# Cross attention's scores as three products of high and low parts instead of one f32 product

## The reference

```python
kv = (mem @ mem_w_kv).astype(jnp.float32)
mem_k = kv[..., :D_MODEL].reshape(B, MEM_LEN, XATTN_HEADS, XATTN_HD)   # 4 heads of 256
mem_v = kv[..., D_MODEL:].reshape(B, MEM_LEN, XATTN_HEADS, XATTN_HD)

def memory_cross_attn(x, mem_k, mem_v, wq, wo):
    q = (x @ wq).reshape(B, S, XATTN_HEADS, XATTN_HD).astype(jnp.float32)
    s = jnp.einsum('bshd,bmhd->bhsm', q, mem_k) * (XATTN_HD ** -0.5)
    p = jax.nn.softmax(s, axis=-1)
    o = jnp.einsum('bhsm,bmhd->bshd', p, mem_v).reshape(B, S, D_MODEL)
    return o @ wo
```

## Time and profile before

| | us |
|---|---|
| median of 3 runs | 960.01 |
| lowest, highest | 959.79, 960.27 |
| run that was profiled | 960.27 |
| its span, from the first to the last instruction | 958.4 |
| TensorE busy | 945.1 (99%) |
| VectorE busy | 685.7 (72%) |
| ScalarE busy | 517.9 (54%) |
| GpSimd busy | 54.5 (6%) |

### The profile page before, as it was taken

The page is one execution under the profiler, slowest core; times in us unless marked ns, Lnnn a source line. Parts: engine busy times, 40 slices in busy tenths (PEclk is TensorE's granted clock), DMA queues, the critical chain, the costliest instruction groups (busy, mean ns, idle before and its releaser), DMA issues.

```text
span 958.4 us, 12980 instructions
## 1 busy us (share of the span) xinstructions
PE 945.1 (99%) x5064; PEld 811.6 (85%) x5064; DVE 685.7 (72%) x933; ACT 517.9 (54%) x732; POOL 54.5 (6%) x96
## 2 busy tenths in 40 slices
PE   9999999999999999999999999998999999999997
PEld 8889888888888888888788888887988888888885
DVE  6966578658888775975788777668677886556555
ACT  6756563526655555264275555547466575444543
POOL 0000121001000002100100000002100000000000
PEclk9999999999999999999999999999999999999998
DMA  9975275527989885183299798763631565655521
GB/s 330 330 252 176 88 273 203 206 88 258 336 273 300 288 289 206 50 312 127 88 317 332 272 305 290 245 224 131 229 130 47 176 223 195 216 179 186 176 78 45
DMA packets 109516, 203.00 MB, mean 212 GB/s; under 512 B 4188, under 2 KB 75120, under 8 KB 106128
## 3 DMA queue, kind: packets, MB, share of 16 engines
q1 hardware_dynamic: 105856, 189.15, 58.2%
q0 software_dynamic: 3168, 12.24, 3.6%
q10 hardware_dynamic: 432, 0.79, 0.2%
HBM read 201.09 MB, written 1.06 MB: 211 GB/s over the span
## 4 chain that ended last, share of the span: by engine, by line
PE 90%; DVE 6%; ACT 2%; issue 1%; DMA 1%; POOL 0%; SPq 0%; POOLq 0%; DVEq 0%; ACTq 0%
PE WB L362 20%; PE YB L387 11%; PE YB L380 10%; PE YB L395 10%; PE WB L365 10%; PE YB L441 4%; PE WB L380 2%; PE WB L344 2%; PE WB L387 2%; PE WB L395 2%; PE WB L351 2%; PE WB L347 2%; PE WB L696 1%; PE WB L715 1%; PE WB L479 1%
## 5 line engine op out<-in xcount | busy, mean ns | idle before, releaser
L1713 DVE TENSOR_TENSOR wl<-raw,wh 128x2048 fp32r<-128x2048 f32 (+1 forms) x146 | 334.3, 2296 | 117.6 <-ACT wh L1103 115.2
L1103 ACT CAST wh<-raw 128x2048 fp32r<-128x2048 f32 (+1 forms) x150 | 285.3, 1905 | 33.7 <-PE YB L395 8.9
L362 PE MATMUL WB<-XS,wh 128*128 128x512 f32 x832 | 208.1, 392 | 0.0
L362 PEld LDWEIGHTS WB<-XS,wh 128*128 128x128 f32 x832 | 152.2, 188 | 29.1
L365 PEld LDWEIGHTS WB<-XS,wl 128*128 128x128 f32 x832 | 113.5, 190 | 8.2
L365 PE MATMUL WB<-XS,wl 128*128 128x256 f32 x832 | 116.0, 282 | 0.0
L380 PE MATMUL YB<-wh,FHT 128*128 128x512 f32 x352 | 109.0, 391 | 0.0
L387 PE MATMUL YB<-wl,FHT 128*128 128x512 f32 x352 | 108.6, 390 | 0.0
L395 PE MATMUL YB<-wh,FLT 128*128 128x512 f32 x352 | 108.5, 389 | 0.0
L1279 ACT COPY U<-WB 128x256 f32<-128x256 f32 x102 | 33.1, 376 | 132.8 <-PE WB L365 132.8
L387 PEld LDWEIGHTS YB<-wl,FHT 128*128 128x128 f32 x352 | 66.1, 188 | 14.1
(11 more groups left out here) (339 smaller groups left out, 1205.8 us busy)
## 6 DMA issues: line engine op xcount, KB each, us to landing
raw<-in_mlp_w SPq DMA_DIRECT2D x64, 1024.0 KB, 5.2
raw<-in_w_ada_t SPq DMA_DIRECT2D x24, 1024.0 KB, 4.9
raw<-in_mlstm_w_in SPq DMA_DIRECT2D x11, 1024.0 KB, 9.0
raw<-in_w_ffn_down SPq DMA_DIRECT2D x11, 1024.0 KB, 5.0
raw<-in_w_ffn_gate SPq DMA_DIRECT2D x10, 1024.0 KB, 5.4
raw<-in_w_ffn_up SPq DMA_DIRECT2D x10, 1024.0 KB, 5.6
raw<-in_mem_w_kv SPq DMA_DIRECT2D x8, 1024.0 KB, 5.2
raw<-in_xattn_wq SPq DMA_DIRECT2D x8, 1024.0 KB, 7.1
```

What stands on the lines that cost most here:

```text
L362: e.matmul(W[:, :], H[:, at(k)], XS[:, k, :], start=k == 0, stop=False)
L1103: f = e.copy(w[:, 0:a * b], raw[:, 0:a * b])
L1713: f = e.tensor_tensor(L[:, 0:a * b], raw[:, 0:a * b], H[:, 0:a * b].bitcast(F32), ALU.subtract)
```

## The change

Scores are computed from high and low parts: high query by high key, high query by low key, low query by high key, all in fp32r and added up in one PSUM bank. For that

- the keys are kept as `KH` and `KL_` in the place of `KV` (a new name `KHL` of type fp32r for the same memory). ScalarE's copy of the keys becomes a cast into `KH`; VectorE computes `KL_` by a new subtraction from the bank (`key_low`, line 1881 of the new file), and it is this that gives the bank back. `VM` moves to columns 2048 to 4095 of `AR`, two bias buffers to columns 4096 to 6143;
- ScalarE's copy of the queries of heads 0 and 1 becomes a cast into `FH`; those of heads 2 and 3 get a new cast behind the join (`high`, line 1312). VectorE gets a new subtraction for each head (`query_low`, line 2055);
- on ScalarE the copy of the turned head 1 stands ahead of the exponentials of head 2; on VectorE the conversion of the third `wo` chunk (`q(3)`) stands behind the scores of head 3.

```diff
-        KT = KV[:, 0:2048].rearrange("p (k c) -> p k c", k=8)
-        VM = KV[:, 2048:4096].rearrange("p (t c) -> p t c", t=2)
+        KH, KL_ = (KHL[:, 2048 * n:2048 * n + 2048].rearrange("p (k c) -> p k c", k=8) for n in range(2))
+        VM = AR[:, 2048:4096].rearrange("p (t c) -> p t c", t=2)
...
@@ TensorE
                 def scores(h):
                     W = bank(("xs", i, h))
-                    e.wait_ge(*act_mlstm["mv", 1, 1])
-                    e.wait_ge(*(act_xa if h < 2 else dve_xa)["q", i, h])
-                    Q = halves(QT[h])
+                    e.wait_ge(*dve_mlstm["mk", 3])
+                    e.wait_ge(*act_xa["qh", i, h])
+                    H, L = halves(FH[h % 2]), halves(FL[h % 2])
                     for t in range(2):
+                        o, tk = W[:, 256 * t:256 * t + 256], slice(128 * t, 128 * t + 128)
                         for f in range(2):
-                            p = e.matmul(W[:, 256 * t:256 * t + 256], Q[:, f, 128 * t:128 * t + 128],
-                                         KT[:, 2 * h + f, :], start=f == 0, stop=f == 1)
+                            e.matmul(o, H[:, f, tk], KH[:, 2 * h + f, :], start=f == 0, stop=False)
+                        for f in range(2):
+                            e.matmul(o, H[:, f, tk], KL_[:, 2 * h + f, :], start=False, stop=False)
+                        e.wait_ge(*dve_xa["ql", i, h])
+                        for f in range(2):
+                            p = e.matmul(o, L[:, f, tk], KH[:, 2 * h + f, :], start=False, stop=f == 1)
                     p.then_inc(pe_xa.add(("s", i, h)))
...
@@ ScalarE
-                e.copy(KT[:, 2 * j:2 * j + 2, :], halves(W[:, :])).then_inc(act_mlstm.add(("mk", j)))
-                freed["mk", j] = act_mlstm["mk", j]
+                e.copy(KH[:, 2 * j:2 * j + 2, :], halves(W[:, :])).then_inc(act_mlstm.add(("mk", j)))
...
-                        e.copy(QT[h], W[:, :]).then_inc(act_xa.add(("q", i, h)))
+                        e.copy(FH[h], W[:, :]).then_inc(act_xa.add(("qh", i, h)))
...
+                def high(h):
+                    e.wait_ge(*dve_xa["q", i, h])
+                    e.wait_ge(*pe_xa["s", i, h - 2])
+                    e.copy(FH[h % 2], QT[h]).then_inc(act_xa.add(("qh", i, h)))
...
                 hi_to(M["wq", i, 3] + 3)
+                high(2)
                 scores(0)
                 q(3)
                 turned(0)
                 scores(1)
+                high(3)
+                turned(1)
                 scores(2)
                 values(0)
-                turned(1)
                 scores(3)
...
@@ VectorE
+            def key_low(j):
+                W = bank_of.get(("mk", j), WB[0])
+                e.wait_ge(*act_mlstm["mk", j])
+                e.tensor_tensor(KL_[:, 2 * j:2 * j + 2, :], halves(W[:, :]),
+                                KH[:, 2 * j:2 * j + 2, :].bitcast(F32), ALU.subtract
+                                ).then_inc(dve_mlstm.add(("mk", j)))
+                freed["mk", j] = dve_mlstm["mk", j]
...
             lo_to(M["mk", 1] + 3)
+            key_low(0)
             head_c(0)
+            key_low(1)
             lo_to(M["mk", 2] + 3)
-            head_a(2)
+            decays(2)
+            key_low(2)
+            weighted(2)
             head_c(1)
             lo_to(M["mk", 3] + 3)
             head_a(3)
             head_c(2)
             lo_to(M["mv", 0, 1] + 3)
+            key_low(3)
             head_c(3)
...
+                def query_low(h):
+                    e.wait_ge(*act_xa["qh", i, h])
+                    e.tensor_tensor(FL[h % 2], QT[h] if h > 1 else YB[2 + h][:, :], FH[h % 2].bitcast(F32),
+                                    ALU.subtract).then_inc(dve_xa.add(("ql", i, h)))
+
-                for h in range(3):
-                    q(h)
+                q(0)
+                query_low(0)
+                q(1)
+                query_low(1)
+                q(2)
                 query(2)
                 scores(0)
-                q(3)
+                query_low(2)
                 query(3)
                 scores(1)
+                query_low(3)
                 scores(2)
                 values(0)
                 scores(3)
+                q(3)
                 values(1)
```

More of the change, by code:

```diff
@@ L182, in build_program @@
         XH, XL = XS[:, :, 0:256], XS[:, :, 256:512]
+        with nc.sbuf_tensor("KHL", [128, 4096], F32R) as KHL:
+            pass
         KV = sb("KV", [128, 4096])
@@ L188, in build_program @@
         FL = [FLT[:, 512 * i:512 * i + 512] for i in range(2)]
-        BV = [sb(f"bv{i}", [128, 1024]) for i in range(2)] + [AR[:, 1024:2048], AR[:, 2048:3072]]
+        BV = [sb(f"bv{i}", [128, 1024]) for i in range(2)] + [AR[:, 4096:5120], AR[:, 5120:6144]]
         IDN = sb("IDN", [128, 128])
@@ L232, in build_program @@
         CT = [S[:, 2 * n:2 * n + 2, :].rearrange("p k c -> p (k c)") for n in range(2)]
-        KT = KV[:, 0:2048].rearrange("p (k c) -> p k c", k=8)
-        VM = KV[:, 2048:4096].rearrange("p (t c) -> p t c", t=2)
+        KH, KL_ = (KHL[:, 2048 * n:2048 * n + 2048].rearrange("p (k c) -> p k c", k=8) for n in range(2))
+        VM = AR[:, 2048:4096].rearrange("p (t c) -> p t c", t=2)
         TMP = AR[:, 6144:8800]
-        QT = [TMP[:, 512 * n:512 * n + 512] for n in range(2)] + [U[:, 0, 512 * n:512 * n + 512] for n in range(2)]
+        QT = [None, None] + [U[:, 0, 512 * n:512 * n + 512] for n in range(2)]
         PART = [U[:, 1, 512 * n:512 * n + 512] for n in range(2)] * 2
@@ L711, in values @@
                     W = bank(("xv", i, h))
+                    e.wait_ge(*act_mlstm["mv", 1, 1])
                     e.wait_ge(*act_xa["pt", i, h])
@@ L724, in free @@
                 def free(t, nb):
-                    return act_xa["q" if t else "ct", i, nb]
+                    return dve_xa["ql", i, nb] if t else act_xa["ct", i, nb]
                 s_ = f"wo{i}"
```

## The result

The changed kernel takes 963.9 us (median of 5 runs, 962.0 to 964.51), the kernel before beside it 959.99 us: a ratio of 1.0037, with a 95% interval of 1.0027 to 1.0048. It is slower by 3.9 us. The forecast was 964.0 us.

What follows compares the result with a forecast made beforehand. TensorE, busy 945.1 us of a 958.4 us span, was taken as the bound. Scores -2.24, attention waits +0.70, wait at the turn +3.7 and clock +1.8 gave +4.0 us: 964.0 us against the 960.01 us median, range 961.3 to 966.3 us.

Steps and rivals of the forecast that it cites:

- Score products: Scores on TensorE: 12 fp32r products at 0.12 us replace 1.73 us of f32 a head, saving 0.29 us each.
- The switch between f32 and fp32r: TensorE around the scores: each switch costs 0.04 us; head 0 loses one, heads 2 and 3 gain one each.
- Attention: Attention of both layers: scores save 1.12 us a layer, less a new TensorE wait of 0.35 us a layer.
- The wait for the exponentials of head 2: Before the values of head 1, TensorE waits for ScalarE 0.35 us a layer, bounds 0 and 1 us.
- The handovers that were to fit by a little: Attention: low and high query parts ready just in time, taken as 0; a rival had four failing at 0.5 us each.
- The wait at the turn: First turn of `y`: TensorE waits 3.7 us for VectorE's low part of keys 3, bounds 2.9 and 4.0 us.
- The clock: Behind the turn's wait: TensorE falls to 1.2 GHz, costing 1.8 us, bounds 0 and 3.6 us.
- the case that the clock holds: Rival behind the turn: same wait but no low clock stretch, +2.2 us, 962.2 us; chance 0.18.
- 0.57: Chance given to the forecast itself, in which the turn waits and the clock falls: +4.0 us, 964.0 us.
- The delay of VectorE from keys 1: Low part of keys 1 delays VectorE by 0.4 us; TensorE reads nothing of it for several microseconds.
- The sum: Whole kernel: -2.24 + 0.70 + 3.7 + 1.8 = +4.0 us, giving 964.0 us against the median.
- The rival that the turn is not held up: First turn of `y`: keys 3 handed over before 119.4, only the scores remain, 957.8 to 958.5 us; chance 0.07.

Runs made afterwards that it cites:

- the experiment with more of them: Changed kernel with low part of keys 3 early and 16 score products a head instead of 12, high query by low key done twice: 961.86 us, ratio 1.0020.
- The best version: Changed kernel with low keys 3 early, low keys 1 in VectorE's wait for GpSimd, and head 2's maximum and exponentials first: 957.94 us, ratio 0.9979.
- the first experiment: Changed kernel with the low part of keys 3 moved on VectorE from behind two weight conversions to right behind decays(3): 958.79 us, ratio 0.9987.
- behind 1.3 us: Changed kernel with the low part of keys 3 between the two weight conversions instead of behind both: 959.98 us, ratio 1.0001.
- behind 2.6 us: Kernel before, with the bank of keys 3 given back by a two-column VectorE copy behind the two weight conversions: 964.36 us, ratio 1.0045.

## Why the prediction was right

- **Score products.** 0.12 us each, as taken from the keys' row. Right, and the experiment with more of them fits it: by the row 32 more should cost 3.84 us less the 0.7 us of wait that they cover, 3.14 us, and they cost 3.07 us. The best version, in which none of the new waits is left, is 2.1 us under before, close to the 2.24 us of the rows. The Trainium skill (FP8 and Floating Point Precision, section TensorE Precision Notes) counts four passes for an f32 product, by which the saving would have been 3.5 us; the measurement decides against it.
- **The switch between f32 and fp32r.** The 0.04 us given to it were read wrongly. Both kernels have a wide group behind fp32r products that takes 1.84 us and not 1.81 us; in the chain of the kernel before, and in that of the changed one behind the new scores:

```profile
178.14 1.84 PE WB L362 x8
```

```profile
179.86 1.84 PE WB L365 x8
```

So what precedes the group is not what makes the 0.03 to 0.04 us, and no run shows a price of the switch. In the sum the term was 0.08 us.

- **Attention.** Forecast 1.12 - 0.35 = 0.77 us saved a layer, measured 0.73 us. The wait for the exponentials of head 2 came as worked out, and going back to the old order of ScalarE made it longer. The handovers that were to fit by a little did fit: no other new wait of TensorE is there.
- **The wait at the turn.** Forecast 3.7 us with the restart, measured 3.57 us and 0.10 us. The hand-over from VectorE took 0.14 us (`issue` in the chain) and lies within the 3.57 us. Where the clock held behind the same wait, the eight turns took 1.06 us instead of 0.87 us, but the group behind them took 0.93 us instead of 1.02 us. So a restart costs 0.14 + 0.10 = 0.24 us, near the 0.27 us of the forecast.
- **The clock.** Forecast 1.8 us, measured 1.61 us in the trace and 1.8 us by filling the wait. I gave 0.18 to the case that the clock holds; in single executions it seems to hold: one of the five of the changed kernel took 962.0 us, about two microseconds under the others. The median is that of the kind in which it falls.

Here the forecast had some luck. Its argument was one fall, 2.0 us after the last product at the end of the kernel before, by which the fall would come well inside a wait of 3.7 us. In the ten traces of this case that time is 2.0 to 4.3 us, and 2.0 is the shortest. The trace of the first experiment, for one: the last product ends at 950.01, and the clock falls at about 954.34.

```profile
950.00:952.00 2.00, 0.01 (x1) 1.00 0.65 262
...
954.00:955.00 1.00, 0.00 (x0) 0.67 0.32 117
```

In the changed kernel the fall came after 3.7 us, when the wait was just over. With such a spread the two cases stood closer together than 0.57 and 0.18.

The price was taken from the pace at the start of the kernel, as that of the low level. The granted clock of the profile does not show a low level there; the first 3 us of the kernel before:

```profile
0.00:3.00 3.00, 1.82 (x8) 1.00 0.35 107
```

So that reading rested on the pace alone. Behind the turn both are seen: granted 0.50, and 1.71 us for four products of 512 columns, which take 0.91 us at 1.00. The low stretch lasted 3.4 us, where 3.9 us were assumed.

- **The delay of VectorE from keys 1.** The size (0.4 us) was right. The sentence that TensorE reads nothing of it for several microseconds was wrong: it is handed on to ScalarE's copies of the first values, which the second panel waits for. In the changed kernel the long wait covers it. It shows only when that is gone, with 0.25 us of wait in the trace and 0.45 us, uncertain, in the time.
- **The sum.** -1.46 + 3.57 + 0.10 + 1.61 = +3.8 us from the rows, against 3.9 us between the medians. The spans of the two traces differ by only 3.5 us, since the first loads came 0.46 us sooner in the second.

The rival that the turn is not held up needed the low part ahead of the conversions. Made so, the kernel took 958.8 us, just above the 957.8 to 958.5 us given for it; the small wait just named is of that size.

## What to carry to other kernels

When a bank's last reader moves to another engine, look at what stands ahead of the reader in that engine's order, and at who takes the bank next: here 0.69 us of work behind 4.5 us of conversions cost 5.1 us. A stop of TensorE can be paid twice, once as the wait and again in its clock, as behind the waits of 2.6 and 3.6 us here and not behind that of 1.3 us. So shorten such a wait, or keep the engine busy in it. Put small extra work of a second engine into its own waits for a third, and before calling a delay hidden, follow it through every engine to the next taker of a bank.

## What the hardware showed that I had not expected

The fall of the clock is not sure at a given wait. By the times of the runs, behind 1.3 us it held in all 11; behind 2.6 us it fell in three of five; behind 3.6 us in four of five. This fits the ends of the ten traces, where it fell 2.0 to 4.3 us after the last product. A kernel with such a wait has two times, 1.5 to 2 us apart, where the kernel before, in 33 runs, keeps to 959.4 to 961.1 us. And products whose results nobody reads made a kernel faster by 1.8 us.
